# A one-core decoder trunk on Trainium2: the first normalisation and its weights in another order, recurrent rows turned and copied piece by piece, the output product in halves of heads

## The reference, cut to what matters

```python
def rms_norm(x, g):
    y = xf * lax.rsqrt(jnp.mean(xf * xf, axis=-1, keepdims=True) + NORM_EPS)
    return (y * g).astype(x.dtype)
...
def hgrn2_mixer(xn, w_in, w_out, g_norm, lb):
    q, f, i, g = jnp.split(xn @ w_in, 4, axis=-1)
    ...
    o = hgrn2_chunk_scan(heads(jax.nn.silu(q)), heads(key), heads(i), heads(logf))
    o = rms_norm(o.transpose(0, 2, 1, 3), g_norm).reshape(B, S, A_WIDTH)
    return (o * jax.nn.silu(g)) @ w_out
...
xn = rms_norm(h, norm_mix[layer]);  h = h + hgrn2_mixer(xn, ...)
xn = rms_norm(h, norm_ffn[layer]);  h = h + swiglu(xn, ...)
```

## Time and profile before

| | us |
|---|---|
| median of three runs | 1565.04 |
| the profiled execution: time, span | 1564.34, 1562.7 |
| TensorE busy | 1524.3 (98% of the span) |
| VectorE, ScalarE, GpSimd busy | 1130.1, 936.4, 56.7 |
| chain of waits, share on TensorE | 94% |
| mean granted TensorE clock | 0.994 of full speed |

### The profile page before, as it was taken

How to read it: one execution, slowest core, us unless ns; L and a number is a source line. 1 busy time by engine, 2 the same in 40 slices (tenths; PEclk the granted TensorE clock), 3 DMA queues, 4 the chain that set the end, 5 groups by cost and what they waited for, 6 DMA issues and landing times.

```text
span 1562.7 us, 19505 instructions
## 1 busy us (share of the span) xinstructions
PE 1524.3 (98%) x6905; PEld 1183.8 (76%) x6905; DVE 1130.1 (72%) x990; ACT 936.4 (60%) x944; POOL 56.7 (4%) x83
## 2 busy tenths in 40 slices
PE   6999899999999898999999999999999999999998
PEld 5866578888555647888888888888888888888886
DVE  1067545554226846888888888888888888888997
ACT  3422244443213535778778778778778778777775
POOL 2000100000101001000000000000000000000100
PEclk9999999999999999999999999999999999999999
DMA  9632165447595007999999999999999999999994
GB/s 362 246 117 82 52 196 181 166 175 171 200 361 188 1 1 245 384 366 369 394 383 357 393 389 359 393 388 353 393 391 358 394 391 349 396 393 350 398 393 179
DMA packets 213021, 455.51 MB, mean 291 GB/s; under 512 B 9857, under 2 KB 36522, under 8 KB 212970
## 3 DMA queue, kind: packets, MB, share of 16 engines
q1 hardware_dynamic: 206714, 441.50, 77.8%
q0 software_dynamic: 3536, 12.96, 2.1%
q10 hardware_dynamic: 2720, 0.38, 0.1%
HBM read 434.89 MB, written 19.92 MB: 291 GB/s over the span
## 4 chain that ended last, share of the span: by engine, by line
PE 94%; DVE 3%; POOL 1%; issue 1%; DMA 0%; ACT 0%; DVEq 0%; POOLq 0%
PE bank L2058 59%; PE bank L1693 8%; PE bank L1710 4%; PE bank L1599 4%; PE bank L1632 4%; PE bank L1756 3%; PE bank L1925 2%; PE bank L1653 2%; PE bank L1621 2%; PE bank L2078 2%; PE bank L1819 1%; PE bank L1793 1%; DVE small L1299 1%; PE bank L1867 1%; PE bank L1894 1%; POOL small L548 1%
## 5 line engine op out<-in xcount | busy, mean ns | idle before, releaser
L1458 DVE TENSOR_TENSOR w_lo<-ring,w_hi 128x2048 fp32r<-128x2048 f32 x333 | 756.3, 2290 | 104.5 <-ACT w_hi L884 103.8
L884 ACT ACTIVATE w_hi<-ring 128x2048 fp32r<-128x2048 f32 x333 | 638.0, 1920 | 168.6 <-PE bank L2058 168.3
L2058 PE MATMUL bank<-w_hi,x_hi 128*128 128x512 f32 x896 | 244.2, 394 | 0.5 <-DVE x_lo L1466 0.5
L2058 PE MATMUL bank<-w_hi,x_lo 128*128 128x512 f32 x896 | 240.0, 390 | 0.0
L2058 PE MATMUL bank<-w_lo,x_hi 128*128 128x512 f32 x896 | 239.7, 389 | 0.0
L2058 PEld LDWEIGHTS bank<-w_hi,x_lo 128*128 128x128 f32 x896 | 168.2, 188 | 35.9
L2058 PEld LDWEIGHTS bank<-w_lo,x_hi 128*128 128x128 f32 x896 | 168.2, 188 | 35.1
L2058 PEld LDWEIGHTS bank<-w_hi,x_hi 128*128 128x128 f32 x896 | 164.5, 188 | 32.1 <-issue 0.7
L1064 DVE TENSOR_TENSOR ring_lo<-ring,f_whi 128x1024 fp32r<-128x1024 f32 x66 | 80.6, 1225 | 76.3 <-ACT f_whi L718 76.3
L2058 PE MATMUL bank<-w_hi,t_hi 128*128 128x512 f32 x448 | 122.6, 395 | 0.0
L2058 PE MATMUL bank<-w_hi,t_lo 128*128 128x512 f32 x448 | 121.1, 392 | 0.0
(11 more groups left out here) (277 smaller groups left out, 1488.4 us busy)
## 6 DMA issues: line engine op xcount, KB each, us to landing
ring<-in_moe_w_gu SPq DMA_DIRECT2D x224, 1024.0 KB, 7.7
ring<-in_moe_w_down SPq DMA_DIRECT2D x112, 1024.0 KB, 7.6
ring<-in_ffn_w_gu SPq DMA_DIRECT2D x22, 1024.0 KB, 6.8
ring<-in_hgrn_w_in SPq DMA_DIRECT2D x16, 1024.0 KB, 14.3
ring<-in_ffn_w_down SPq DMA_DIRECT2D x10, 1024.0 KB, 6.8
x_rows<-arena SPq DMA_DIRECT2D x2, 4096.0 KB, 21.2
ring<-in_kv_w SPq DMA_DIRECT2D x6, 1024.0 KB, 6.2
ring<-in_hgrn_w_out SPq DMA_DIRECT2D x4, 1024.0 KB, 8.2
```

Source lines behind the costliest of these rows:

```text
L884: act.activation(w_hi[s % PARTS][:, :], raw[:, s % RAWS, :], ACT.Copy).then_inc(hi_ready, 1)
L1458: dve.tensor_tensor(w_lo[s % PARTS][:, :], raw[:, s % RAWS, :], w_hi[s % PARTS][:, :].bitcast(F32), ALU.subtract).then_inc(lo_ready, 1)
L2058: last = mm(out_, x_[k], w[:, k, 512 * b:512 * b + 512], start=start and k == 0 and n == 0, stop=stop and k == HALF // width - 1 and n == 2)
```

## The change

Start: the six norm-weight transfers go to ScalarE's queue, ahead of its first work, so that SyncE issues the ring's weights right after x. GpSimd, VectorE and TensorE no longer wait for the masks; GpSimd issues their transfer only after the constants have landed, and waits for them after the first norm. TensorE turns the norm weights before the rows of x, and VectorE copies them before it scales x. `transposed` tells after each bank, and the first projection waits bank by bank. Output: each piece is turned alone, all four copies are ScalarE's, and the first quarter of the output product is cut in two halves of heads, each behind its own copy. The remaining lines only count the semaphores `xT_dve` and `xT_act` anew.

```diff
-            g = arena[:, 0:128]
-            for k, (w, r) in enumerate(((norm_mix, G_MIX0), (norm_ffn, G_FFN0))):
-                sp.dma_start(g[r:r + 16, :], w.rearrange("l (k p) -> (l k) p", p=P)).then_inc(gain_in, 16)
...
             pool.dma_start(cf[:], const_f32).then_inc(const_in, 16)
             masks = arena[:, 2048:2048 + (MLEV + 1) * P]
-            pool.dma_start(masks, const_masks).then_inc(const_in, 16)
-            pool.wait_ge(const_in, 32)
+            pool.wait_ge(const_in, 16)
...
+            pool.dma_start(masks, const_masks).then_inc(const_in, 16)
             norm(0)
+            pool.wait_ge(const_in, 32)
...
             step = Steps(act, act_step)
+            g = arena[:, 0:128]
+            for k, (w, r) in enumerate(((norm_mix, G_MIX0), (norm_ffn, G_FFN0))):
+                act.dma_start(g[r:r + 16, :], w.rearrange("l (k p) -> (l k) p", p=P)).then_inc(gain_in, 16)
...
-                last.then_inc(xT_act, 1)
+                    last.then_inc(xT_act, 1)
...
+            o_squared(0)
+            o_squared(1)
+            o_squared(2)
+            o_turned(0)
+            o_squared(3)
+            o_turned(1)
+            o_turned(2)
+            o_turned(3)
...
-            norm(0)
             dve.wait_ge(gain_in, 96)
...
             step(dve.tensor_scalar(gnar[0:DH, GQ:GQ + 1], gnar[0:DH, GQ:GQ + 1], float(DH) ** -0.5, None, ALU.mult))
+            norm(0)
             transposed(G_MIX0)
...
-                if j >= 2:
-                    tb = j - 2
-                    dve.wait_ge(oT_ps, 2 * tb + 1)
-                    dve.tensor_scalar(a_oT[:, 0:4, P * tb:P * tb + P],
...
-            norm()
             pe.wait_ge(gain_in, 96)
             pe.wait_ge(gains_ps, 1)
             tp(bank[:, 4, 0:R_GAIN], arena[0:R_GAIN, 0:P], ident[0:R_GAIN, 0:R_GAIN])
             tp(bank[0:DA, 4, 64:68], arena[0:4, 128:128 + DA], ident[0:4, 0:4]).then_inc(gains_ps, 1)
-            pe.wait_ge(xT_dve, 1)
-            pe.wait_ge(xT_act, 1)
+            norm()
...
+                        if j == 0 and hh == 0 and k % 2 == 0:
+                            pe.wait_ge(xT_act if k % 4 else xT_dve, k // 4 + 1)
...
+            recurrent_out(2)
+            o_turn(0)
+            recurrent_out(3)
+            pe.wait_ge(oT_act, 1)
+            pe.wait_ge(osq_ready, 1)
+            pe.wait_ge(on_ready, 1)
+            out_hgrn(0, range(0, 4))
+            o_turn(1)
+            pe.wait_ge(oT_act, 2)
+            out_hgrn(0, range(4, 8))
             pe.wait_ge(on_ready, 2)
...
+            o_turn(2)
             out_hgrn(1)
+            o_turn(3)
+            pe.wait_ge(oT_act, 4)
             out_hgrn(2)
```

More of the change, by code:

```diff
@@ L293, in trunk @@
             sem(n) for n in ("dist_ready", "fac_ready", "ops_ready", "pair_ps", "pair_taken", "zeroed"))
-        o_ps, osq_ready, oss_ready, ors_ready, on_ready, oT_ps, oT_dve, oT_act = (
-            sem(n) for n in ("o_ps", "osq_ready", "oss_ready", "ors_ready", "on_ready", "oT_ps", "oT_dve", "oT_act"))
+        o_ps, osq_ready, oss_ready, ors_ready, on_ready, oT_ps, oT_act = (
+            sem(n) for n in ("o_ps", "osq_ready", "oss_ready", "ors_ready", "on_ready", "oT_ps", "oT_act"))
         sg_ready, res_ps = sem("sg_ready"), sem("res_ps")
@@ L638, in _ @@
             step = Steps(act, act_step)
+            g = arena[:, 0:128]
+            for k, (w, r) in enumerate(((norm_mix, G_MIX0), (norm_ffn, G_FFN0))):
+                act.dma_start(g[r:r + 16, :], w.rearrange("l (k p) -> (l k) p", p=P)).then_inc(gain_in, 16)
+            act.dma_start(g[G_KV:G_KV + 8, :], kv_norm.rearrange("(k p) -> k p", p=P)).then_inc(gain_in, 16)
+            act.dma_start(g[G_HG:G_HG + 1, :], hgrn_g_norm).then_inc(gain_in, 16)
+            act.dma_start(arena[GQ:GQ + 1, 128:128 + DH], nsa_q_norm).then_inc(gain_in, 16)
+            act.dma_start(arena[GK:GK + 3, 128:128 + DH], k_norm).then_inc(gain_in, 16)
             def squared(i, tb, count, junk=None):
@@ L701, in _, with o_squared @@
             act.activation(a_sg[:, :, :], a_sg[:, :, :], ACT.Silu).then_inc(sg_ready, 1)
-            for j in range(4):
+            def o_squared(j):
                 act.wait_ge(o_ps, j + 1)
@@ L705, in _, with o_turned @@
                 act.activation(a_sq[:, j, :], bank[:, j, :], ACT.Square).then_inc(osq_ready, 1)
-            for tb in range(TB):
-                act.wait_ge(oT_ps, 2 * tb + 2)
-                act.activation(a_oT[:, 4:8, P * tb:P * tb + P], bank[:, 5 + 2 * tb, :].rearrange("p (k t) -> p k t", k=4),
-                               ACT.Copy, scale=gain[:, G_HG:G_HG + 1]).then_inc(oT_act, 1)
+            def o_turned(j):
+                tb, grp = divmod(j, 2)
+                act.wait_ge(oT_ps, j + 1)
+                act.activation(a_oT[:, 4 * grp:4 * grp + 4, P * tb:P * tb + P],
+                               bank[:, 4 + j, :].rearrange("p (k t) -> p k t", k=4),
+                               ACT.Copy, scale=gain[:, G_HG:G_HG + 1]).then_inc(oT_act, 1)
+            o_squared(0)
[6 more added lines that the diff above has]
+            o_turned(3)
             quarters = [0]
@@ L958, in _ @@
             step = Steps(dve, dve_step)
-            dve.wait_ge(const_in, 32)
             def norm(i):
@@ L974, in transposed @@
                                                  gain[:, g0 + k:g0 + k + 1], None, ALU.mult)
-                last.then_inc(xT_dve, 1)
-            norm(0)
+                    last.then_inc(xT_dve, 1)
             dve.wait_ge(gain_in, 96)
@@ L1051, in _ @@
                                   ALU.mult).then_inc(on_ready, 1)
-                if j >= 2:
-                    tb = j - 2
-                    dve.wait_ge(oT_ps, 2 * tb + 1)
-                    dve.tensor_scalar(a_oT[:, 0:4, P * tb:P * tb + P],
-                                      bank[:, 4 + 2 * tb, :].rearrange("p (k t) -> p k t", k=4),
-                                      gain[:, G_HG:G_HG + 1], None, ALU.mult).then_inc(oT_dve, 1)
             quarters = [0]
@@ L1558, in _ @@
             mm, tp = nc.tensor.matmul, nc.tensor.transpose
-            pe.wait_ge(const_in, 32)
+            pe.wait_ge(const_in, 16)
             def turn_block(src, tb, k0, b, told):
@@ L1637, in _, with recurrent_out @@
             pe.wait_ge(qv_taken, 12)
-            for j in range(4):
+            def recurrent_out(j):
                 tb, grp = divmod(j, 2)
@@ L1656, in out_hgrn, with o_turn @@
                         last.then_inc(res_ps, 1)
-            pe.wait_ge(on_ready, 2)
[L1659 to L1666, removed]
+            def o_turn(j):
+                pe.wait_ge(on_ready, j + 1)
+                turn_block(a_on, j // 2, 4 * (j % 2), 4 + j, oT_ps)
+            recurrent_out(0)
+            recurrent_out(1)
+            recurrent_out(2)
[8 more added lines that the diff above has]
+            out_hgrn(0, range(4, 8))
+            pe.wait_ge(on_ready, 2)
+            o_turn(2)
             out_hgrn(1)
-            pe.wait_ge(oT_act, 2)
-            pe.wait_ge(oT_dve, 2)
+            o_turn(3)
+            pe.wait_ge(oT_act, 4)
             out_hgrn(2)
@@ L1677, in _ @@
             out_hgrn(3, range(4, 8))
-            pe.wait_ge(xT_dve, 4)
+            pe.wait_ge(xT_dve, 5)
             def parts(d, width):
@@ L1735, in _ @@
                     if n == 0 and a == 2:
-                        pe.wait_ge(xT_dve, 5)
+                        pe.wait_ge(xT_dve, 6)
                     gu_quarter(n, a)
@@ L1768, in _ @@
                 if j < 2:
-                    pe.wait_ge(xT_dve, 6 + j)
-                    pe.wait_ge(xT_act, 2 + j)
+                    pe.wait_ge(xT_dve, 7 + j)
+                    pe.wait_ge(xT_act, 3 + j)
                 shared(j)
-            pe.wait_ge(xT_dve, 9)
-            pe.wait_ge(xT_act, 5)
+            pe.wait_ge(xT_dve, 10)
+            pe.wait_ge(xT_act, 6)
             pe.wait_ge(misc_in, 80)
```

## The result

The changed kernel takes 1557.0 us (median of five runs, 1555.5 to 1558.7) against 1565.04. The ratio is 0.9948, 95% interval 0.9935 to 0.9962, so 8.0 us faster by the medians. Timed again later (E10) it took 1556.1, ratio 0.9939 (0.9926 to 0.9953). The profiled execution took 1556.34 us, its span is 7.9 us shorter than before.

What follows compares the result with a forecast made beforehand. TensorE was taken as the bound, so only its waits and slow stretches counted. Front 3.8 plus output stage 4.8 made 8.6 us off, 1555.7 from the profiled run or 1556.4 from the median; forecast 1556.2, range 1553.0 to 1560.8.

Steps and rivals of the forecast that it cites:

- Front, part 1: Start of the kernel: constants land at 7.8, contention priced 0.8 us (0 to 1.6), first normalisation of x 0.4 us earlier.
- Front, part 2: First transpose to projection: norm weights turned during the earlier wait, copies awaited piece by piece; 2.6 us gained.
- The cover for the norm weights: Start: turning and copying norm weights, from 7.8 to 8.8, is hidden by the wait for the normalisation at 9.43.
- The first slot's cover: Before the projection: the first 2.1 MB of weights land by 12.5, leaving 1.7 us to spare.
- Front, part 3: First projections: the slow clock stretch behind the removed idle costs 1.7 us; half, 0.8, taken as gain (ends 0 and 1.7).
- Output stage: Output product: early turns and halves bring it 4.8 us sooner (ends 4.0 and 5.2), clock 3.1, new waits 0.85 each.
- Cover of the residuals: After the output product: residual sums are ready at 192.0, TensorE asks at 193.0, leaving 1.0 us.
- The sum: Whole kernel: front 3.8 us plus output stage 4.8 us give 8.6 us saved.
- everything comes 4 us earlier against whatever the clock looks at: Output-stage rival: the clock falls there, price 3.1 us, total 1559.3; chance 0.18 together with longer waits.
- Norm weights late: Front rival: norm weights land at 12.2, front gives nothing, 1560.2; at 14.8, about 1562.8; chance 0.13.

Runs made afterwards that it cites:

- E10: The changed kernel itself timed once more, against the kernel before; 1556.07 us, ratio 0.9939.
- E8: E7's kernel with the masks issued behind the first norm's inverse roots and norm-weight copies put between the first two row blocks; 1553.12 us, ratio 0.9924.
- E4: The changed kernel with the six norm-weight transfers back on SyncE between x and the weights; 1557.13 us, ratio 0.9947.
- E1: The front's part of the change alone on the kernel before, output stage as before; 1560.5 us, ratio 0.9968.
- E5: The changed kernel with unread identity transposes filling TensorE's waits at the last pair products, in attention and in the routing; 1557.16 us, ratio 0.9953.
- E6: The changed kernel with the output product's first quarter in one piece behind both pieces' turns and copies; 1557.57 us, ratio 0.9954.
- E7: The changed kernel with the second piece turned right behind the last recurrent products and the fourth right behind the third; 1555.13 us, ratio 0.993.
- E2: The output stage's part of the change alone on the kernel before, front as before; 1563.38 us, ratio 0.999.
- E3: The kernel before with 15 and 18 unread identity transposes filling TensorE's waits ahead of the output product; 1563.51 us, ratio 0.9991.

## Why the prediction was right

The forecast was 1556.2 us, 1557.0 came. By its steps:

- **Front, part 1.** 0.4 us forecast, 0.7 measured. The constants landed at 7.17, not 7.8, 0.1 us later after their issue than in the profile before. Over all profiles they took 5.2 to 5.5 us where the weights were issued behind the norm weights and 5.5 to 5.9 where they were not, so the price is some 0.3 us, near the lower end, and halfway was too much. GpSimd issued the masks 0.3 us after the landing, which I had not counted.
- **Front, part 2.** 2.6 forecast; first transpose to projection took 3.67 instead of 6.47, 2.8. The cover for the norm weights was thinner than I wrote: turned and copied by 9.0, not 8.8, with the normalisation due at 9.1. In E10, the same kernel, the last norm weights are let through at 8.11 and the chain runs through them, so this cover was about used up. E8 had to move the copies before it could start earlier. The first slot's cover is real and small: E4 is held by it.
- **Front, part 3.** 0.8 forecast. In the profiled run 57.21 - 55.39 = 1.8. The other profiles with this front have 56.55 (E1), 56.50 (E5), 55.96 (E6), 55.49 (E7) and 55.31 us (E10), so the gain is 0.7 to 1.9, 1.3 in the mean of the six, between the half that I took and the upper end of 1.7. The suspicion that the transposes run slowly under a granted clock of 1.00 fits the durations: 421 ns each in the front against 273 at 170 us, and the first projections in E1 and E8 are slow as well.
- **Output stage.** 4.8 forecast, 4.3 measured (35.4 to 31.0 us from the first recurrent output product to the residual's turns). The first half came 3.9 us sooner as forecast; waits took 0.78, not 0.85; but in the chain a run of products behind a wait takes 0.26 us more (3.70 for 3.44, 7.13 for 6.87), twice. The quarter's 3.1 us at the lower clock were the larger part of it in this pair of profiles, and moving turns and copies the other 1.2. The runs bear only a part of this out: the stage's edit gave 2.0 us alone (E2) and 3.2 beside the new front (mean spans 1558.2 of E1 and 1555.1), not 4.8, because slow stretches came at other places.
- **Cover of the residuals**: 1.0 forecast, 1.5 there.
- **The sum** was right partly by luck. The two stages gained 9.8 us in this profile, 1.2 more than forecast (front 1.6 more, output stage 0.5 less), and 1.9 went back, nearly all through a clock fall in attention. I had "everything comes 4 us earlier against whatever the clock looks at" as a rival for the output stage only, at 3.1 us; E2 and E3 show it at the recurrence's tail, E2 and E4 near 456, the changed kernel at 501.5, and every profile in the routing. It is no rival outcome but a term of every run (clock loss 6.5 to 9.7 us in the means of the two kernels, of which a part is standing and costs nothing), and the forecast should have had it with both signs.
- **Norm weights late**: their reader goes at 7.86, far from 12.2, so they did not each wait behind a large piece of the weights.

What stays open: which stretches a given run loses. The same idle of 2.1 us at the tail cost nothing in the profiles of before, of the changed kernel, of E1, E6, E8 and E10, and was followed by the lower clock in those of E2, E3, E4 and E7; and E2 and E4 had a fall behind work without a wait. I did not find out what sets it. So the idle removed at the front and the new order of turns are shown as causes of their share; that the filled or removed waits are what kept the clock up is argued from single profiles.

## What to carry to other kernels

Where TensorE is the bound, look for short waits followed by slow records: there the wait's price is the wait and what the slow records take beyond their fast time (3.1 us for the quarter here), and the second part comes and goes between runs. Turn and copy piece by piece as soon as a piece is ready, and put the next turn ahead of the current product, so its copy has cover; cutting the product itself bought little (E6: 0.6 us in the trace). Before speeding up a stretch, see who waits at its end: in the routing the time went into a wait for VectorE. A gain of a few us must be read over several runs beside the mean clock, since one profile may have won or lost as much by chance; and the mean clock itself is not time.

## What the runs showed of the hardware

- The granted clock of the profile read 1.00 at the program's start while the records were slow: in E8 the first three projections took 754, 634 and 551 ns, later ones 379; in the kernel before such records took 634 under a reading of 0.57. Durations, not the clock row, tell the speed there.
- With unread transposes of 0.11 us each in a wait, the products behind it ran at full speed (E3: 7.10 us for a quarter instead of 9.94; E5: 1.08 for eight records instead of 1.82); E2 and E8 had the same at these places without them. Where the clock was already down they took 0.2 each and overran (E5, 3.45 us for 16).
- A fall of the clock without a wait ahead of it: 0.50 at 457.8 to 461 in E2, TensorE busy throughout (3.20 of 3.20 us, and the 18 us before).
- 303.5 KB of constants landed in 5.5 to 5.9 us with the weights issued from 1.89 us on beside them (eight profiles), in 5.2 to 5.5 with the weights issued from 4.1 on (four, three of them with the masks beside them as well): some 0.3 us for the contention that I had put at 0 to 1.6.
- Six norm-weight transfers of 8 KB and less on ScalarE's queue: the last, issued at 3.17, let its reader go 4.7 us later, beside x and the weights. On SyncE's queue, ahead of the weights (E4), the last was issued at 3.80 and let its reader go 3.8 us later.
